# When the next pass's token rows are transposed and rounded in an expert loop

## The reference, cut to what matters

```
def expert_block(args):                     # 128 token rows idx of one expert e
    xb = t[idx]
    hu = xb @ w1[e] + b1[e]                 # 1024 x 2048
    glu = jnp.minimum(hu[:, 0::2], SWIGLU_LIMIT)
    lin = jnp.clip(hu[:, 1::2], -SWIGLU_LIMIT, SWIGLU_LIMIT)
    act = glu * jax.nn.sigmoid(SWIGLU_ALPHA * glu) * (lin + 1)
    return act @ w2[e] + b2[e]              # 1024 x 1024
```

## Time and profile before

| | us |
|---|---|
| median of 3 runs (range) | 2899.38 (2894.09 to 2905.55) |
| the profiled execution's own time | 2905.33 |
| its span | 2903.7 |
| PE busy in the span | 2588.8 (89%) |
| DVE busy in the span | 1972.8 (68%) |
| ACT busy in the span | 1503.8 (52%) |

### The profile page before, as it was taken

How to read it: one execution, slowest core, us unless ns; L and a number is a source line. 1 busy time by engine, 2 the same in 40 slices (tenths; PEclk the granted TensorE clock), 3 DMA queues, 4 the chain that set the end, 5 groups by cost and what they waited for, 6 DMA issues and landing times. The chain is left out here.

```text
span 2903.7 us, 39975 instructions
## 1 busy us (share of the span) xinstructions
PE 2588.8 (89%) x12446; PEld 1990.8 (69%) x12447; DVE 1972.8 (68%) x2924; ACT 1503.8 (52%) x1834; POOL 487.6 (17%) x419
## 2 busy tenths in 40 slices
PE   7999969999799229999999999999999999999970
PEld 2475559999654117777777777777777777777750
DVE  2531257777633628777877777687777777899968
ACT  3210146666522026665666666566656656677751
POOL 1000013222211340210111021112102110222210
PEclk9999979999898569999999999999999999999985
DMA  9640053334322058877887787788778878999988
GB/s 326 158 137 30 1 130 79 83 79 93 109 93 92 15 173 283 307 259 257 296 297 239 276 308 272 244 294 310 249 262 300 292 241 283 327 376 373 375 301 303
DMA packets 301499, 647.53 MB, mean 223 GB/s; under 512 B 14610, under 2 KB 15874, under 8 KB 301298
## 3 DMA queue, kind: packets, MB, share of 16 engines
q1 hardware_dynamic: 279586, 574.63, 58.2%
q0 software_dynamic: 21872, 72.38, 7.6%
HBM read 606.47 MB, written 46.56 MB: 225 GB/s over the span
## 5 line engine op out<-in xcount | busy, mean ns | idle before, releaser
L1545 DVE TENSOR_TENSOR w_lo_x<-wring_x,w_hi_x 128x2048 fp32r<-128x2048 f32 x446 | 1014.7, 2283 | 58.9 <-issue 33.0
L1459 ACT ACTIVATE w_hi_x<-wring_x 128x2048 fp32r<-128x2048 f32 x448 | 849.8, 1907 | 16.1 <-DMA wring_x<-in_w_mlp 15.6
L1691 PE MATMUL psum<-w_hi_x,x_hi_x 128*128 128x512 f32 x1184 | 497.1, 420 | 4.3 <-DVE w_lo_x L1545 4.3
L1693 PE MATMUL psum<-w_hi_x,x_lo_x 128*128 128x512 f32 x1184 | 463.7, 392 | 0.0
L1692 PE MATMUL psum<-w_lo_x,x_hi_x 128*128 128x512 f32 x1184 | 463.0, 391 | 0.0
L1422 POOL TENSOR_TENSOR poolgate_x<-poolgate_x 128x1 f32<-128x1 f32 x74 | 75.4, 1019 | 1182.7 <-DVE y_x L1578 678.4
L1691 PE MATMUL psum<-w_hi_x,a_hi_x 128*128 128x512 f32 x592 | 249.8, 422 | 14.9 <-DVE a_lo_x L1606 14.9
L1691 PEld LDWEIGHTS psum<-w_hi_x,x_hi_x 128*128 128x128 f32 x1184 | 225.0, 190 | 48.3 <-DVE w_lo_x L1545 9.0
L1693 PEld LDWEIGHTS psum<-w_hi_x,x_lo_x 128*128 128x128 f32 x1184 | 222.9, 188 | 49.1
L1692 PEld LDWEIGHTS psum<-w_lo_x,x_hi_x 128*128 128x128 f32 x1184 | 224.0, 189 | 43.1
L1693 PE MATMUL psum<-w_hi_x,a_lo_x 128*128 128x512 f32 x592 | 231.2, 391 | 0.0
(11 more groups left out here) (301 smaller groups left out, 3985.6 us busy)
## 6 DMA issues: line engine op xcount, KB each, us to landing
wring_x<-in_w_mlp SPq DMA_DIRECT2D x448, 1024.0 KB, 6.8
bias<-bias_d SPq DMA_DIRECT2D x32, 640.0 KB, 8.1
late<-in_w_ada SPq DMA_DIRECT2D x32, 512.0 KB, 3.8
yg<-y_d SPq DMA_DIRECT2D x8, 2048.0 KB, 10.9
ring<-in_w_ada SPq DMA_DIRECT2D x4, 2048.0 KB, 8.5
ring<-in_w_in SPq DMA_DIRECT2D x4, 2048.0 KB, 9.8
ring<-in_w_out SPq DMA_DIRECT2D x2, 2048.0 KB
mix_d<-o SPq DMA_DIRECT2D x16, 256.0 KB, 2.0
```

Of the source, the lines that this page charges most:

```text
L1459: act.activation(w_hi[:, n % HI, k, :], ring[:, n % RING, k, :], ACT.Copy).then_inc(hi_done, 1)
L1545: dve.tensor_tensor(w_lo[:, n % LO, k, :], ring[:, n % RING, k, :], w_hi[:, n % HI, k, :].bitcast(F32), ALU.subtract).then_inc(lo_done, 1)
L1691: pe.matmul(bank, hi[:, k, :], w_hi[:, n % HI, k, :], start=False, stop=False)
L1693: last = pe.matmul(bank, lo[:, k, :], w_hi[:, n % HI, k, :], start=False, stop=(k == KD - 1))
```

## The change

Only the places of three calls are changed; all instructions, their operands and their semaphores stay.

- PE: the 8 transposes of the next rows' first block (`rows(nxt, 0)`) stood before the second layer's first product. Now they stand inside that product right behind `columns` of the last activation: between the halves in a single pass, after the product in a double one.
- ACT: `x_hi` of those rows stood before the `w_hi` half and `a_hi`. Now it stands behind `a_hi` (in a double pass behind the 64-row block's `a_both`).
- DVE: `x_lo` stood before `a_lo`. Now it stands behind it.

The second block's rows of a double pass (`rows(nxt, 1)`) stay where they were.

```diff
@@ ACT, body @@
-                    if ups <= j < ups + next_r:
+                    if ups < j < ups + next_r:
                         rows(nxt, j - ups)
...
                     piece(ahead[1], r)
                     if 1 <= j <= ups:
                         columns(st, j - 1)
+                    if j == ups:
+                        rows(nxt, 0)
@@ PE @@
-            def product(st, j, bank, hi, lo, both):
+            def product(st, j, bank, hi, lo, both, nxt):
...
                     if c and before and not is_half(st, (j - 1) % st.R):
                         columns(st, j - 1)
+                        if j == UP * st.R:
+                            rows(nxt, 0)
...
                 if before and is_half(st, (j - 1) % st.R):
                     columns(st, j - 1)
+                    if j == UP * st.R:
+                        rows(nxt, 0)
...
-                    product(st, j, ps[:, j % 2, :], x_hi, x_lo, x_both)
-                rows(nxt, 0)
+                    product(st, j, ps[:, j % 2, :], x_hi, x_lo, x_both, nxt)
```

More of the change, by code:

```diff
@@ L1723, in body @@
                     pe.matmul(bank, sel_down[:, r, :], btab[:, 2 * FF + h * UNIT:2 * FF + (h + 1) * UNIT], start=True, stop=False)
-                    product(st, ups + i, bank, a_hi, a_lo, a_both)
+                    product(st, ups + i, bank, a_hi, a_lo, a_both, nxt)
                     if i + 1 < next_r:
```

## The result

| | before | changed |
|---|---|---|
| median, us (6 runs each) | 2898.34 | 2882.28 |
| range, us | 2894.09 to 2905.55 | 2879.56 to 2887.89 |
| profiled execution's span, us | 2903.7 | 2886.1 |

The ratio is 0.9945, 95% interval 0.9929 to 0.9962: 0.55% or 16 us less, where 17.8 us and 2882 were forecast. The spans differ by 17.6 us.

The account below looks back on a forecast made before the run. The prediction took PE to set the pace in the passes, with its wait for `a_lo` leading. 14 x 1.10 = 15.4 plus 2.4 from late passes made 17.8 us off 2899.38: 2881.6 us, range 2869 to 2899.

Parts of the forecast that it names:

- What bounds the kernel: In the passes PE sets the pace; its leading wait is for `a_lo` at slice 6, 14 times, 14.9 us.
- PE, single pass: In a pair's single pass PE reaches slice 6 at 1507.09 instead of 1508.22, gaining 1.10 us, 14 times.
- DVE and ACT: In a pair's single pass `a_lo` follows `w_lo` directly, `a_hi` ends by 1506.1, and `a_lo` ends at 1507.03.
- PE's move: The 8 transposes move into the second layer's first product, 0.87 us at either place; PE reaches the activation's transposes sooner.
- Late single passes: In 8 late single passes nothing is waited for any more: 0.30 us gained each, 2.4 us in all.
- What comes late instead: `x_lo` starts 1.0 us later in late passes; `w_lo` half 1 stays covered, by 0.9 us there, 1.9 in double passes.
- Double pass: No wait to remove at its last activation, the 64-row block's: total 0, bounds -0.1 and +0.1 each.
- The sum: 15.4 + 2.4 = 17.8 us off all passes, from a median of 2899.38 to 2881.6, 0.61% less.
- The count by starts: PE's loss at 14 seams is 19.5 us by matmul starts, against 14.9 of listed idle time; the forecast uses starts.
- Rival A: Late passes give the gain back through later ring loads, up to 1.0 us each: 2886 to 2892, chance 26%.
- B: Slower: `w_lo` half 1 behind the delayed `x_lo` in DVE's queue holds up PE: 2913, chance 7%.
- C: Nothing gained: at the seam PE's wait only moves from `a_lo` to `act_o`: 2899, chance 5%.

Follow-up runs that it names:

- reads_before: Kernel before, with DVE's two expert-table reads moved behind the first two `w_lo` halves in single passes: 2887.33 us, ratio 0.9939.
- two padded runs: Changed kernel with one or three useless DVE subtractions ahead of `a_lo` in single passes: 2892.41 and 2920.05 us.
- pe_only: Kernel before with only PE's transposes moved, ACT and DVE left as before: 2963.36 us, ratio 1.0222.
- xhi_late: Changed kernel with ACT's `x_hi` one `w_hi` half later in single passes: 2915.11 us, ratio 1.0050.

## Why the prediction was right

*What bounds the kernel.* Right that the wait for `a_lo` was the place. "So in the passes PE sets the pace, and a change pays only by what it takes out of PE's own line" is wrong for a pair's single pass: DVE sets the pace there, and PE follows it closely. The busy times of the pair hide it, since they average over the double pass. The single pass alone, before (columns as in the earlier trace rows):

```profile
1476.61:1516.28 39.67, 37.82 (x176) 29.52 (x176) 35.01 (x34) 30.06 (x26) 10.42 (x9) 1.00 0.95 332
```

PE is busy for 95% of it and DVE for 88%, where the pair has 98 and 77%. `reads_before` and the two padded runs show who follows whom. The forecast didn't suffer, because it followed DVE's queue up to `a_lo` as well as PE's, and both came to the same time for slice 6, 1507.09. The 1.14 us that `x_lo` had taken in DVE's queue is in fact what the pass lost, to 0.02.

*PE, single pass.* 1.10 us expected, 1.12 measured (39.67 - 38.55), 14 times. The touch with `act_o` came as read, and the wait for `a_lo` is gone.

*DVE and ACT.* `a_lo` directly behind `w_lo` with `a_hi` in time: shown, and the two orders are now priced apart, 0.75 and 0.37.

*PE's move.* I took it as a part of how the gain comes about and gave it no price of its own. It has none beside the other two parts: 38.55 and 36.11 us with and without it. Alone it is a loss (`pe_only`). For the sum it made no difference.

*Late single passes.* 0.30 expected, 0.27 measured; the 1.0 us that `a_lo` has to spare there was confirmed by the two padded runs.

*What comes late instead.* The wait ahead of `x_lo`, 1.0 us expected, is 0.88 in late passes and 1.33 in double ones. `w_lo` half 1 behind it starts about 1.0 us later in late passes and 1.7 in double ones, as worked out, and PE never waits for it. But "Nobody needs `x_lo` until the next pass" was wrong, and it is the one step that could have cost something. In a pair's single pass the second block's transposes need it. There `x_lo` now ends at 1502.90 + 1.23 = 1504.13, and PE starts these transposes at 1504.47: a cover of 0.34 us that stands nowhere in my working. It held, which was luck: with `x_hi` some 1.8 us later, in `xhi_late`, each of these passes lost 1.56 us.

*Double pass.* 0 expected; 60.67 us before and 60.69 now.

*The sum.* The 36 passes are 17.8 us shorter (1704.9 - 1687.1), which is the number forecast. 14 x 1.12 = 15.7 and 7 x 0.27 = 1.9 are 17.6 of it, the first pass 0.25. The medians say 16 us, within their interval of 11 to 21.

*The count by starts.* The listed idle time of 14.9 us alone would have given 14 us and nothing in late passes. Measured were 17.8, with 0.27 in each late pass, in which the trace of before listed no wait at all. The rule cited from the Trainium skill (Perfetto Trace Analysis, section "Tensor Engine Instruction (MATMUL, LD_WEIGHTS)"), that a matmul's end in a profile is an estimate, agrees with this case.

*Rival A* did not happen. Its first link may have: in late passes ACT waits for its ring more than before (6.1 us, 12 times, from 2510 to 2780 us in the changed kernel, against 2.9 us, 6 times, from 2510 to 2800 in the one before). Each is a single execution, and over all the runs these waits come to anything between 0.5 and 19 us. None of it reaches PE. *B* needed a longer delay, which `xhi_late` gave it. *C* is excluded by the touch's price of 0.1 us.

## What to carry to other kernels

In an engine's queue, sort the instructions of a step by who is waiting: what the bound engine needs within this step goes ahead of what is needed in the next one, and then ask for each move who reads the moved result, the buffers that it frees included. An engine that is 77% busy over a pair of passes, and 88% in the single pass within, can set the pace there while another shows 95%: add some dead work to its queue, and if the stretch grows one to one, every microsecond taken out of that chain is a gain, wherever in it, until another engine's own work is the longer. When a change has several parts, take them apart; here DVE's part alone gave two thirds of the gain, ACT's on top of it the last third, and PE's nothing beside them and a loss of 65 us alone.

## What was not expected of the hardware

The granted clock of TensorE fell in some late passes of `pe_only`, to 0.92 and 0.86 of full speed over stretches of 10 and 7 us, which is some 3 us of matmuls at 1.2 GHz instead of 2.4. It followed waits of 2.25 us, of the same length in passes where the clock did not fall. In one pass of `reads_before` it fell to 0.83 over 10 us behind a wait of 1.80 us. Waits of 1.8 to 2.25 us in PE can so cost another 1.6 us, and here mostly did not.

DVE's two reads of a register value from memory took 1.44 of the 2.33 us of idle time where its queue was empty, and behind the two `w_lo` halves they cost nothing. The profile puts the other 0.89 down to DVE's own last result. But inside the double pass the same two instructions, `y` and then `w_lo`, stand only 0.34 us apart:

```profile
1566.08 4.49 DVE L1545 TENSOR_TENSOR w_lo_x<-wring_x,w_hi_x 128x2048 fp32r<-128x2048 f32 x2 [0.34 <-DVE y_x L1578]
```

So some 0.55 us of it belong to the step from one pass to the next.
